# PEER experts: low parts of U and V made in four pieces on GpSimd, and the products with low parts placed last in each dot and each sum

## What is computed

```python
def one(tb):                                    # a block of tokens
    q = (tb @ wq).reshape(PEER_BLOCK, PEER_HEADS, 2, PEER_QDIM // 2)
    s = jnp.einsum('thcd,hcnd->thcn', q, keys)
    sv, si = lax.top_k(s, PEER_TOPK)
    ...                                         # e: 16 experts per head, g: their softmax weights
    a = jax.nn.gelu(jnp.einsum('td,thkd->thk', tb, u_tab[e]), approximate=False)
    return jnp.einsum('thk,thkd->td', g * a, v_tab[e])
```

## Time and profile before

| | |
|---|---|
| median of three runs | 4121.95 us (4121.81, 4121.95, 4129.34) |
| profiled execution, its own time | 4132.75 us |
| its span | 4130.9 us |
| experts stage, first to last matmul | 2104 to 4045 us of the span |
| TensorE busy / VectorE busy / GpSimd busy | 3358.8 us (81%) / 2775.2 us (67%) / 1710.3 us (41%) |
| granted TensorE clock, whole span | 0.90 of full speed |

### The profile page before, as it was taken

How to read it: one execution, slowest core, us unless ns; L and a number is a source line. 1 busy time by engine, 2 the same in 40 slices (tenths; PEclk the granted TensorE clock), 3 DMA queues, 4 the chain that set the end, 5 groups by cost and what they waited for, 6 DMA issues and landing times. The chain is left out here.

```text
span 4130.9 us, 59356 instructions
## 1 busy us (share of the span) xinstructions
PE 3358.8 (81%) x20729; PEld 2933.1 (71%) x20729; DVE 2775.2 (67%) x5874; ACT 1352.9 (33%) x3186; POOL 1710.3 (41%) x1341
## 2 busy tenths in 40 slices
PE   6799678565776886466669999999999999999995
PEld 3577455211466786355569999999999999999994
DVE  3114586200024059999968999889899989998885
ACT  3000366100022111578723333333333333333331
POOL 1001000000030432678855556556655655655550
PEclk8899899778678998667779999999999999999997
DMA  6766544799522332254578898889888888988984
GB/s 232 256 223 221 166 151 134 304 408 415 213 87 74 96 107 81 62 117 111 123 257 314 315 332 324 310 315 327 316 309 324 320 320 319 328 318 302 330 286 154
DMA packets 389553, 1001.91 MB, mean 243 GB/s; under 512 B 187044, under 2 KB 232975, under 8 KB 325688
## 3 DMA queue, kind: packets, MB, share of 16 engines
q1 hardware_dynamic: 323768, 491.18, 35.0%
q0 software_dynamic: 62656, 469.86, 31.5%
q10 hardware_dynamic: 2944, 38.77, 2.6%
HBM read 914.75 MB, written 152.04 MB: 258 GB/s over the span
## 5 line engine op out<-in xcount | busy, mean ns | idle before, releaser
L2163 DVE CUSTOM_DVE_ANT_0 e_uv<-e_uv,e_h 128x1024 f32<-128x1024 f32 x416 | 717.2, 1724 | 86.4 <-DMA e_uv<-peer_uv,k_g_idx 85.2
L2232 POOL DMA_INDIRECT e_uv<-peer_uv,k_g_idx x416 | 520.2, 1251 | 547.4 <-DVE e_pY L2175 503.1
L1470 PE MATMUL e_po<-e_ph,e_vh 128*128 128x320 f32 x2048 | 646.8, 316 | 55.9 <-DVE k_OT L2207 49.5
L1470 PE MATMUL e_pa<-k_hi_d,e_uh 128*128 128x320 f32 x2048 | 640.4, 313 | 59.7 <-POOL e_ul L2223 43.3
L1472 PE MATMUL e_pa<-k_hi_d,e_ul 128*128 128x320 f32 x2048 | 634.4, 310 | 0.0
L1471 PE MATMUL e_pa<-k_lo_d,e_uh 128*128 128x320 f32 x2048 | 634.3, 310 | 0.0
L1472 PE MATMUL e_po<-e_ph,e_vl 128*128 128x320 f32 x2048 | 634.0, 310 | 0.0
L1471 PE MATMUL e_po<-e_pl,e_vh 128*128 128x320 f32 x2048 | 634.0, 310 | 0.0
L2175 DVE SCALAR_TENSOR_TENSOR e_pY<-e_uv,e_wts,e_pY 128x1024 f32<-128x1024 f32 x412 | 525.8, 1276 | 0.0
L1470 PEld LDWEIGHTS e_po<-e_ph,e_vh 128*128 128x128 f32 x2048 | 385.5, 188 | 79.0 <-DVE k_OT L2207 64.9
L1470 PEld LDWEIGHTS e_pa<-k_hi_d,e_uh 128*128 128x128 f32 x2048 | 385.9, 188 | 73.0 <-issue 51.8
(11 more groups left out here) (301 smaller groups left out, 5974.9 us busy)
## 6 DMA issues: line engine op xcount, KB each, us to landing
s_kv<-kv_pages SPq DMA_DIRECT2D x128, 512.0 KB, 6.8
s_kv<-kv_state SPq DMA_DIRECT2D x32, 2048.0 KB, 17.3
e_v<-peer_uv SPq DMA_DIRECT2D x128, 512.0 KB, 6.4
e_u<-peer_ut SPq DMA_DIRECT2D x126, 512.0 KB, 6.1
s_g<-r_G SPq DMA_DIRECT2D x10, 4096.0 KB, 21.1
k_OT<-s_g SPq DMA_DIRECT2D x128, 320.0 KB, 5.7
k_win_sample<-state_k_win ACTq DMA_DIRECT2D x28, 1168.0 KB
v_win_sample<-state_v_win POOLq DMA_DIRECT2D x28, 1168.0 KB, 9.8
```

Source lines behind the costliest of these rows:

```text
L1470: nc.tensor.matmul(out, lhs_hi, rhs_hi, start=start, stop=False)
L2163: nc.vector.tensor_tensor_reduce(uv[:, r, 0:D], uv[:, r, 0:D], h[:], 1.0, 0.0, ALU.mult, ALU.add, dots[:, r:r + 1]).then_inc(row_dotted, 1)
L2232: nc.gpsimd.indirect_dma_start(uv[:, s % RING], None, io["peer_uv"], bass.IndirectOffsetOnAxis(ap=keep.g_idx[:, s:s + 1], axis=0),).then_i ...
```

## The change

Three edits, all in `peer_experts`.

1. GpSimd makes each low part in four pieces of 128 x 256 instead of one of 128 x 1024. The semaphore is counted up by the last piece alone.
2. TensorE's products are reordered. In a block the 16 matmuls with the high part of U come first and the 8 with its low part last; a chunk starts when the high part is there (`uh_done`), and ahead of the first low product of the chunk it waits for `ul_done`. In a sum the four matmuls of high times high come first, then four with the low part of V, then four with the low part of the activations; `out` starts on `vh_done`, and waits for `vl_done` ahead of the first low product of V, that is after 4 matmuls instead of ahead of all; the activations' high and low parts have waits of their own.
3. ScalarE issues `split_u` of chunks 2 and 3 right behind the gelu of blocks 1 and 3, ahead of the wait for `p_done` and of the copy to `e_ph`, instead of behind that copy.

The number of matmuls, their shapes, the DMAs and the order on VectorE and SyncE stay.

```diff
@@ TensorE
                 def dot(i, c):
-                    pe.wait_ge(ul_done, CQ * i + c + 1)
+                    pe.wait_ge(uh_done, CQ * i + c + 1)
                     for b in range(NBD):
                         m = NBD * c + b
                         pe.wait_ge(p_done, DOTS * i + m + 1)
                         cols = slice(b * WD, (b + 1) * WD)
                         for k in range(KC):
-                            x = split_product(nc, pa[:, m % 2, 0:WD], uh[:, c % 2, k], ul[:, c % 2, k],
-                                              keep.hi_d[:, k, cols], keep.lo_d[:, k, cols], k == 0, k == KC - 1)
+                            nc.tensor.matmul(pa[:, m % 2, 0:WD], uh[:, c % 2, k], keep.hi_d[:, k, cols], start=(k == 0), stop=False)
+                            nc.tensor.matmul(pa[:, m % 2, 0:WD], uh[:, c % 2, k], keep.lo_d[:, k, cols], start=False, stop=False)
+
+                        if b == 0:
+                            pe.wait_ge(ul_done, CQ * i + c + 1)
+                        for k in range(KC):
+                            x = nc.tensor.matmul(pa[:, m % 2, 0:WD], ul[:, c % 2, k], keep.hi_d[:, k, cols], start=False,
+                                                 stop=(k == KC - 1))
                         x.then_inc(dotted, 1)
                 def out(i):
-                    pe.wait_ge(vl_done, CQ * i + CQ)
+                    pe.wait_ge(vh_done, CQ * i + CQ)
...
-                        pe.wait_ge(pl_done, DOTS * i + NBD * (CQ - 2) + b + 1)
+                        pe.wait_ge(ph_done, DOTS * i + NBD * (CQ - 2) + b + 1)
...
                             for c in range(CQ):
                                 if k == 0 and c == CQ - 1:
-                                    pe.wait_ge(pl_done, DOTS * i + NBD * (CQ - 1) + b + 1)
-                                x = split_product(nc, po[:, n % SUMS, 0:WD], vh[:, c, k * P:(k + 1) * P],
-                                                  vl[:, c, k * P:(k + 1) * P], ph[:, c, cols], pl[:, c, cols],
-                                                  c == 0, c == CQ - 1)
+                                    pe.wait_ge(ph_done, DOTS * i + NBD * (CQ - 1) + b + 1)
+                                nc.tensor.matmul(po[:, n % SUMS, 0:WD], vh[:, c, rows], ph[:, c, cols], start=(c == 0), stop=False)
+
+                            if n == 0:
+                                pe.wait_ge(vl_done, CQ * i + CQ)
+                            for c in range(CQ):
+                                nc.tensor.matmul(po[:, n % SUMS, 0:WD], vl[:, c, rows], ph[:, c, cols], start=False, stop=False)
+                            if k == 0:
+                                pe.wait_ge(pl_done, DOTS * i + NBD * (CQ - 1) + b + 1)
+                            for c in range(CQ):
+                                x = nc.tensor.matmul(po[:, n % SUMS, 0:WD], vh[:, c, rows], pl[:, c, cols], start=False,
+                                                     stop=(c == CQ - 1))
                             x.then_inc(summed, 1)
@@ ScalarE
                     nc.scalar.activation(pa[:, m % 2, 0:WD], pa[:, m % 2, 0:WD], ACT.Gelu).then_inc(gelu_done, 1)
+                    if b == 1 and c < 2:
+                        split_u(CQ * i + 2 + c)
                     act.wait_ge(p_done, n + 3)
...
                         gelus(i, m)
-                        if m % NBD == 1 and m // NBD < 2:
-                            split_u(CQ * i + 2 + m // NBD)
                         if m in V_AT:
@@ GpSimd
                 def low_u(c):
                     pool.wait_ge(uh_done, c + 1)
-                    nc.gpsimd.tensor_tensor(ul[:, c % 2], uu[:, c % 2], uh[:, c % 2], ALU.subtract).then_inc(ul_done, 1)
+                    for n in range(PIECES):
+                        k = slice(n * KC // PIECES, (n + 1) * KC // PIECES)
+                        x = nc.gpsimd.tensor_tensor(ul[:, c % 2, k], uu[:, c % 2, k], uh[:, c % 2, k], ALU.subtract)
+                    x.then_inc(ul_done, 1)
```

7 lines of the change are left out of this document (6 added, 1 removed).

## The result

The changed kernel takes 4266.4 us (median of 4 runs, 4263.4 to 4268.5) against 4123.5 us on the same chip: ratio 1.034, 95% interval 1.033 to 1.036. It is slower by about 143 us. The forecast was 4165 with a range up to 4225: the direction held, the size didn't, and the time lies outside the range.

The account below looks back on a forecast made before the run. TensorE was taken to bound the stage, with GpSimd's chain just in time. Matmuls 56.3, low part of V 3.4, clock 1.0, sums half 0.8, small 0.2 make 61.7 against 60.3 us a round: 4165 us, range 4060 to 4225.

Parts of the forecast that it names:

- TensorE sets the stage: Experts stage: matmuls take 56.3 of 60.3 us a round, so edits of waits can bring about 125 us in all.
- second chain with no room: GpSimd's low parts, 2843.91 to 2864.78 in the round shown, end just as TensorE could begin the sums half, 2864.6.
- Length of a piece: GpSimd: a 256-column piece takes 0.70 to 0.72 us; four take 2.85 against 2.41 us, 0.45 more.
- Who gets in between: Boundaries of GpSimd's pieces: VectorE gets in at most of them and gains perhaps 5 of its 10.2 us a round.
- faster rival: VectorE gains and GpSimd hardly pays: 58.8 us a round, 4076 us; chance 0.33.
- What GpSimd pays: GpSimd's dots half: VectorE operations meeting low parts add 3.5 us; the chain takes 26.0 and ends at 32.2 us.
- 1.3 off: Start of GpSimd's chain: first low part of V begins 6.2 instead of 7.56 us into the round, as VectorE catches up.
- The waits for e_ul "go": TensorE's new order: low part of U needed 2.3 us later, so its waits, 0.65 us a round plus refill, vanish.
- have their slots a chunk ahead: SyncE's loads follow the low parts, come up to 0.45 us later, and were taken to have slots a chunk ahead.
- Part 3's price: Earlier split_u: GpSimd's idle 1.11 us goes, but its low part now meets VectorE's dot and low part of activations.
- five meetings: GpSimd's dots half: three VectorE dots and two low parts of activations fall into low parts, 3.5 us, bounds 0 and 5.
- The sum: Per round: 56.3 + 3.4 + 1.0 + 0.8 + 0.2 = 61.7 us against 60.3, so +43 us over 31 rounds.

Follow-up runs that it names:

- less_whole: Kernel before, with GpSimd's low parts cut to 768 of 1,024 columns from the second round on, each in one operation: 4050.7 us, ratio 0.982.
- pieces_alone: Kernel before, with only the low parts of U and V made in four pieces on GpSimd: 4241.5 us, ratio 1.026.
- after_loads: Changed kernel, with SyncE issuing both loads of U ahead of the waits and loads of V: 4263.0 us, ratio 1.032 against the kernel before.

## Why the prediction was right and wrong

- **What bounds the kernel.** The pace of the matmuls held: 384 matmuls at 0.147 us are 56.4 us in both kernels. But "TensorE sets the stage" was only part of it: `less_whole` gains 2.7 us a round, two thirds of all that TensorE stood, from less work on GpSimd and the 6.6 us that VectorE is then held up less. Neither of the two is full (GpSimd idles 24 us of 60, VectorE 6.0); the prediction's own "second chain with no room" describes it better.
- **Length of a piece.** 0.70 to 0.72 us forecast, 0.70 measured (2.80 for four). Right.
- **Who gets in between.** Forecast "at most boundaries", VectorE gains 5 us a round: its holding up fell from 10.2 to 6.1 in the changed kernel and to 4.4 in `pieces_alone`. Right in size. What it is worth was overrated in the faster rival: the case that hung on VectorE's 10.2 us had 0.33.
- **What GpSimd pays.** Forecast: the chain of six low parts is 20.9 + 2.7 - 1.1 + 3.5 = 26.0 us and ends 32.2 into the round. Measured in the mean: it starts at 8.7, not 6.2, takes 24.7 and ends at 33.4. The "1.3 off" for a VectorE that has caught up didn't come (8.5 before, 8.7 after). The six low parts took 5.8 us more than before, close to the forecast's 2.7 + 3.5; but the three gathers among them took 1.2 us less, which the sum lacked, and the idle time fell by 0.8. Two errors that mostly cancel, so that the end came out near is luck.
- **The waits for e_ul "go".** Wrong. The step looked at the slack of 2.3 us and not at where the longer chain puts `e_ul`: the low part of U for chunk 2 is the second in the chain and ends 18.0 us into the round instead of 15.2. With the old order TensorE then waits 3.9 us (`pieces_alone`), with the new one 1.3.
- **SyncE's loads "have their slots a chunk ahead".** The step that failed outright. In SyncE's row the load of U for chunk 3 stands behind V's first low part, and ScalarE can go on 7.0 us after its issue (2845.70 to 2852.68). With `split_u` moved up, ScalarE stands on it, and with it `e_ph`, `e_pl`, `e_act` and TensorE at matmul 144: 1.7 us a round that are not in the sum. In `after_loads` the stand at 144 is gone and the time comes back at the low part of V and at matmul 336; as the edit costs by itself, how much of the time this error accounts for stays open.
- **Part 3's price.** "They are among the five meetings" took in GpSimd's side of the meeting and not VectorE's: `e_pl` 0.48 to 2.69 us. Alone the moved split costs 0.5%, 0.7 us a round, where the text had a gain of 1.1 us for GpSimd.
- **The sum.** Forecast beside 56.3: 3.4 for the low part of V, 1.0 for the clock, 0.8 in the sums half, 0.2 small. Measured beside 56.4: 1.7 at matmuls 195 and 196 (about half of it for `e_ph` and half for the low part of V), 1.0 for matmuls at half clock, 1.3 in the sums half, 0.3 small, and 3.6 in the dots half, for which the sum had nothing: 0.4 at 48, 1.3 at 112 and 113, 1.9 at 144 and 168. The term that was mis-sized is the dots half. The chain was followed to its end only, and every stand of TensorE along it was left out.
- **The range.** The forecast's own cases ended at 4210; its bounds let the meetings go to 5 us but nothing else. A chain with no room has a price at each place where it is read, and the upper end should have taken these in.

The clock: 1.0 us forecast, 1.0 measured. One stand of 2.73 us at the low part of V (3381.63 above) is followed by this stretch, columns as in the earlier trace rows:

```profile
3381.70:3384.80 3.10, 3.10 (x16) 3.10 (x17) 2.65 (x4) 1.45 (x3) 2.75 (x3) 0.70 1.01 398
```

at 0.70 of the full clock, partly at 1.2 instead of 2.4 GHz; before it was the earlier trace rows. Some 260 matmuls between 2200 and 4150 us started while the granted clock stood at 0.5, against some 40 in the stage before.
